# A two-layer diffusion trunk step: the end of the expert routing and the first expert, reordered

## The chip, the cores and the metric

The kernel runs on one core of one Trainium2 chip. The metric is the device time of one execution in microseconds (us); less is better. The core has a matrix engine (TensorE, PE in the rows, with its weight loads shown apart as PEld), a vector engine (VectorE, DVE), an activation engine (ScalarE, ACT), a general engine (GpSimd, POOL) and a queue engine (SyncE, SP). Each engine runs its own list of instructions in order; semaphores order them against each other. SP and POOL also start DMA transfers between the chip's memory (DRAM) and the on-chip memories.

## The reference

Two layers; each has a mixer (attention, in layer 0 beside a recurrent branch) and then an expert-choice mixture of experts with 16 experts. The change touches the mixture in both layers. 1024 latent tokens and 128 context tokens pass through the same experts in separate calls: an expert takes its 128 best latent tokens and its 16 best context tokens.

```python
def ec_moe(h, p):
    B, L, D = h.shape
    n = B * L
    cap = EC_FACTOR * n // N_EXPERTS
    xt = h.reshape(n, D)
    aff = jax.nn.softmax(jnp.matmul(xt, p['router'], preferred_element_type=jnp.float32), axis=-1)
    gate, idx = lax.top_k(aff.T, cap)
    xe = jnp.take(xt, idx, axis=0)
    hid = jax.nn.silu(jnp.einsum('ecd,edf->ecf', xe, p['w_gate'])) * jnp.einsum('ecd,edf->ecf', xe, p['w_up'])
    ye = jnp.einsum('ecf,efd->ecd', hid, p['w_down']) * gate[..., None].astype(h.dtype)
    out = jnp.zeros_like(xt).at[idx.reshape(-1)].add(ye.reshape(-1, D))
    return out.reshape(B, L, D)

def trunk_layer(x, cond, p, mixer, ctx, rope):
    sh1, sc1, g1, sh2, sc2, g2 = adaln(cond, p['ada_w'], p['ada_b'])
    mix, state = mixer(modulate(rms_norm(x, p['norm1']), sh1, sc1), p, ctx, rope)
    x = x + g1 * mix
    x = x + g2 * ec_moe(modulate(rms_norm(x, p['norm2']), sh2, sc2), p)
    return x, state
```

## The kernel before

The kernel is a row of stages. A stage is one block with a hand-written instruction list for each engine; it ends when all five engines have ended their lists. Per layer the last three stages are `mixer_out`, `routing` and `experts`.

**routing.** VectorE finds the top lists: first the context tokens' (semaphore `topped` 1), then the latent ones' in 16 rounds (`topped` 2). TensorE turns the two lists (L2164, L2165); VectorE writes them to `idx` and `gate`, and POOL gathers expert 0's 128 token rows from DRAM into `x_next` (L2022). Beside that, TensorE forms part of layer 1's modulation in `block_sums` (`ada.partial`, L260, and `ada.turn`, L248) from `ada` weights that SP loads; with `l == 0` there are ten such blocks, and the weights lie where expert weights will lie (slots 4 to 11 of `raw`). TensorE also builds the context tokens' inputs (L2153, `x_ctx`), spreads the gate vector g2 over all rows (`spread_g2`, L2131, 32 products with the identity, in the accumulator's banks 0 to 3), which ScalarE copies out (L2199), and starts expert 0's context products (`first_ctx_gu`).

**experts.** An expert's gate and up weights come in eight row blocks k of 1 MiB (`load_gu`, slots 0 to 7 of `raw`, each as two transfers of 512 KB), its down weights in four of 1 MiB (`load_dn`, slots 8 to 11). A slot is split into a high part (ScalarE, `copy_high`, L2060) and a low part (VectorE, `subtract_high`, L2063, which overwrites `raw`); TensorE then does 12 products per slot: a unit, `lat_gu` (L2449) or `lat_dn` (L2464), counted by `lat_done`. When unit k is done, SP loads the next expert's block into the slot. The context tokens use the unsplit weights: `ctx_gu` (L2051) does 32 products on four blocks of `raw`, so an expert has two halves; `ctx_dn` (L2431) does 64 on the down weights. These steps count `ctx_done`, and `low` on VectorE waits for it before it overwrites `raw`. Between them lie `turn_ctx` (L2411, transposes of the context products), `silu_ctx` on ScalarE and `hid_ctx` on VectorE. `turn_x` (L2392) transposes gathered rows, `turn_hid` (L2402) an expert's hidden rows. The loop `body(b)` runs expert b's down products and expert b+1's gate and up products.

The order in TensorE's list for expert 0, before the first `body`:

```python
            turn_x(0)
            for k in range(KB):
                lat_gu(0, k, k)
                if k == 1:
                    turn_x(1)
                    if l == 0:
                        ctx_gu(0, 1)
                if k == 5:
                    ctx_gu(1, 0)
            body(0)
```

In `body`, after the unit with k == 1, come `turn_hid(b)`, `turn_ctx(b)`, `ctx_gu(b + 1, 1)` and `ctx_dn(b)`. POOL splits expert 1's rows (`split_x`, L2342 and L2344), gathers expert 2's and then lays out expert 1's context inputs (`place_ctx`, L2044) with `l == 0`; with `l == 1` it lays them out before the split.

Of the kernel before, what the change touches and what calls it, by code (L numbers as in the profile page):

```python
# [1986 lines left out]
def moe_memory(m, a, sem, l, x_lat, h_at, hi_at, y_ctx_dram):  # L1987
# [79 lines left out]
    mm.n_low = (1, 2)[l]  # L2067
# [3 lines left out]
def routing(nc, m, a, sem, l, mm, dram, ada):  # L2071
# [16 lines left out]
    with nc.Block() as block:  # L2088
        @block.sync
        def _(sp):  # L2090
            ada.ahead(sp, (7, 3)[l])
            ada.loads(sp, (14, 0)[l])
            for k in range(4 if l == 0 else KB):
                mm.load_gu(sp, k, 0)
            if l == 1:
                for i in range(4):
                    if i < 1:
                        ada.wait_free(sp, 3 + i)
                    mm.load_dn(sp, i, 0)
# [21 lines left out]
        @block.tensor  # L2121
        def _(pe):
            def first_ctx_gu():
                pe.wait_ge(mm.s["padded"], 1)
                pe.wait_ge(mm.s["xc_ready"], 1)
                mm.ctx_gu(pe, 0, 0)

            def spread_g2():
                for c in range(2):
                    for k in range(KB):  # L2130
                        last = pe.matmul(m.psum[:, 2 * c * BANK + k * P:2 * c * BANK + (k + 1) * P],  # L2131
                                         m.mod[l][:, 5 * KB + k, c:c + 1].broadcast_to([P, P]), m.ident[:, :],
                                         start=True, stop=True)
                    last.then_inc(s["g2_spread"], 1)

            def block_sums(i):
                if i >= done:
                    ada.partial(pe, i)
                if i >= 1:
                    ada.turn(pe, i - 1)  # L2140
                if i == ada.count - 1:
                    ada.turn(pe, i)

            for i in range(early):
                block_sums(i)
            pe.wait_ge(s["sel_ready"], 1)
            for i in range(2):
                last = pe.transpose(m.psum[:, 4 * BANK + 2 * P + i * P:4 * BANK + 2 * P + (i + 1) * P], sel01[:, i, :], m.ident[:, :])
            last.then_inc(s["sel_turned"], 1)
            pe.wait_ge(s["sel_copied"], 1)  # L2150
            for k in range(KB):

                last = pe.matmul(m.psum[:, k * 2 * P:(k + 1) * 2 * P], mm.h_ctx[:, k * P:(k + 1) * P], sel_t[:, :],  # L2153
                                 start=True, stop=True)
            last.then_inc(s["ctx_done"], 1)
            for i in range(early, ada.count):
                block_sums(i)
            pe.wait_ge(s["ctx_read"], 1)
            if l == 1:
                pe.wait_ge(s["mod_ready"], 1)  # L2160
                spread_g2()
                first_ctx_gu()
            pe.wait_ge(s["topped"], 2)
            pe.transpose(m.psum[:, 4 * BANK:4 * BANK + EXP], topf[0:EXP, 0:CAP_L], m.ident[0:EXP, 0:EXP])  # L2164
            pe.transpose(m.psum[:, 4 * BANK + EXP:4 * BANK + 2 * EXP], top[0:EXP, 0:CAP_L], m.ident[0:EXP, 0:EXP]  # L2165
                         ).then_inc(s["top_turned"], 1)
            if l == 1:
                mm.ctx_gu(pe, 0, 1)
            else:
                first_ctx_gu()  # L2170
                spread_g2()

        @block.scalar
        def _(act):
            for i in range(early):
                ada.copy(act, i)
            if l == 1:
                for k in range(2):
                    act.wait_ge(mm.loaded[k], 32)
                    mm.copy_high(act, k)  # L2180
# [16 lines left out]
            for c in range(2):  # L2197
                act.wait_ge(s["g2_spread"], c + 1)
                act.copy(mm.g2[:, c, :], m.psum[:, 2 * c * BANK:(2 * c + 2) * BANK]).then_inc(s["g2_read"], 1)  # L2199
            if l == 1:  # L2200
                act.wait_ge(mm.s["ctx_done"], 2)
                mm.copy_gu_c(act)
# [64 lines left out]
def experts(nc, m, a, sem, l, mm, dram, x_ctx_from, x_ctx_to, tail_loads):  # L2267
# [20 lines left out]
    with nc.Block() as block:  # L2288
        @block.sync
        def _(sp):  # L2290
# [19 lines left out]
            if l == 0:  # L2310
                for k in range(4, KB):
                    mm.load_gu(sp, k, 0)
# [25 lines left out]
        def _(pool):  # L2338
# [17 lines left out]
            def body(b, first=False, more=2):  # L2356
                if not first:
                    scatter(b - 1)
                if more >= 1:
                    wait_value(m, pool, s["ctx_done"], b * 3 + 4)  # L2360
# [6 lines left out]
            if l == 1:  # L2367
                mm.place_ctx(pool, 1)
# [15 lines left out]
        def _(pe):  # L2384
# [83 lines left out]
            def body(b, last=False):  # L2468
                for k in range(KB):
                    lat_gu(b + 1, b * UNITS + (8 + k), k)  # L2470
                    if k == 1:
                        turn_hid(b)
                        turn_ctx(b)
                        ctx_gu(b + 1, 1)
                        ctx_dn(b)
# [12 lines left out]
            turn_x(0)  # L2488
            for k in range(KB):
                lat_gu(0, k, k)  # L2490
                if k == 1:
                    turn_x(1)
                    if l == 0:
                        ctx_gu(0, 1)
                if k == 5:
                    ctx_gu(1, 0)
            body(0)
# [14 lines left out]
        def _(act):  # L2512
# [29 lines left out]
            def read_gu_c(e):  # L2542
                act.wait_ge(s["ctx_done"], e * 3 + 1 if not (isinstance(e, int) and e == 0) else 2)
# [12 lines left out]
            def body(b, last=False):  # L2556
# [14 lines left out]
                silu_ctx(b)  # L2571
# [30 lines left out]
            if l == 0:  # L2602
                read_gu_c(0)
            for k in (6, 7):
                high(k, 32, k - 3)
            for k in (0, 1, 2):
# [3 lines left out]
            body(0)  # L2610
# [7 lines left out]
        def _(dve):  # L2618
# [38 lines left out]
            def body(b, first=False, more=True, last=False):  # L2657
# [5 lines left out]
                hid_ctx(b)  # L2663
                hid_low(b)
                for n in (4, 5, 6, 7):
                    low(unit(n), n, b * 3 + 4)
# [29 lines left out]
            for k in range(4, 8):  # L2696
                low(k, k, 2)
                if k == 5:
                    next_rows(2)
            for k in range(2):  # L2700
# [133 lines left out]
```

## Time and profile before

| what | us |
|---|---|
| median of 3 runs | 3346.57 |
| lowest and highest run | 3341.72 and 3347.82 |
| the profiled execution | 3345.91 |
| its span, first to last instruction | 3344.1 |
| TensorE busy in the span | 3125.9 (93%) |
| VectorE, ScalarE, GpSimd busy | 2259.8, 1887.1, 629.0 |

All times in the rows are from the span's start. Layer 0's routing stage runs from 748.4 to 802, its experts from 802.8; layer 1's routing from 2537.7 to 2585, its experts from 2586. A row of the timeline gives start, duration, engine, line, operation, output and inputs, the number of instructions merged into it, and in brackets the idle time of the engine just before it with what ended that. A merged row runs from the first start to the last end; matmuls overlap, so the time that a step takes is read from its start to the next row's start.

### The profile page before, as it was taken

The page shows a single profiled execution, that of the slowest core. Times are in us where ns is not written, and L with a number is a line of the kernel's source. Part 1 is how long each engine was busy: PE and PEld are TensorE (multiplying, and loading weights), DVE is VectorE, ACT ScalarE, POOL GpSimd, SP SyncE. Part 2 cuts the span into 40 slices and gives each one's busy share as a digit, 9 for nine tenths or more (in the row PEclk, how much of TensorE's full clock was granted, in tenths as well). Part 3 has the DMA queues.
Part 4 walks back from the last instruction along what each step waited for, and adds up shares of the span by engine and source line. Part 5 has one row for each costly group of instructions (what it writes and reads, how often), then busy time and mean ns, then how long its engine had stood idle before and what let it go on. Part 6 is the DMA issues. An engine that isn't in the chain of part 4 may idle for free. (4 is left out here: it accounts for less than half of the span.)

```text
span 3344.1 us, 55681 instructions
## 1 busy us (share of the span) xinstructions
PE 3125.9 (93%) x20174; PEld 2419.7 (72%) x20174; DVE 2259.8 (68%) x2853; ACT 1887.1 (56%) x2677; POOL 629.0 (19%) x484
## 2 busy tenths in 40 slices
PE   6988989988999999997999999999996999999999
PEld 4757878864677776775787888888884667677676
DVE  4667777547566666665687786867757666666666
ACT  3545848434466656664366483855733565566654
POOL 1111010001222233221211111021100222322221
PEclk9989999998999999998999999999997999999999
DMA  6230000349788888886010100100145788888885
GB/s 230 87 129 21 2 22 1 135 168 355 261 308 288 305 285 287 309 288 203 7 42 8 42 5 4 42 7 23 46 164 201 264 302 289 285 306 291 302 287 160
DMA packets 214171, 565.37 MB, mean 169 GB/s; under 512 B 33699, under 2 KB 71272, under 8 KB 213736
## 3 DMA queue, kind: packets, MB, share of 16 engines
q1 hardware_dynamic: 203614, 529.21, 43.8%
q0 software_dynamic: 9472, 33.57, 4.2%
q8 instruction: 110, 1.80, 0.2%
q14 instruction: 69, 0.57, 0.0%
q10 hardware_dynamic: 906, 0.23, 0.0%
HBM read 524.00 MB, written 38.94 MB: 168 GB/s over the span
## 5 line engine op out<-in xcount | busy, mean ns | idle before, releaser
L2063 DVE TENSOR_TENSOR moe_lo<-moe_raw,moeg_hi 128x2048 fp32r<-128x2048 f32 x384 | 883.5, 2328 | 308.3 <-ACT moeg_hi L2060 164.2
L2060 ACT CAST moeg_hi<-moe_raw 128x2048 fp32r<-128x2048 f32 x384 | 729.2, 1911 | 460.0 <-PE psum L2449 338.7
L1090 PE MATMUL psum<-attn_w_hi,attn_hs 128*128 128x256 f32 (+2 forms) x1440 | 375.0, 344 | 30.5 <-PEq L2726 14.6
L1575 DVE TENSOR_REDUCE attn_neg_max<-psum 128x1 f32<-128x1280 f32 (+1 forms) x216 | 292.5, 1354 | 86.5 <-PE psum L1196 85.4
L1196 PE MATMUL psum<-attn_ks,attn_qst 128*128 128x512 f32 (+2 forms) x1200 | 313.1, 377 | 21.8 <-ACT attn_e L1356 12.4
L1356 ACT ACTIVATE attn_e<-psum,attn_neg_max 128x1280 f32<-128x1280 f32 (+1 forms) x216 | 264.8, 1226 | 75.8 <-DVE attn_neg_max L1575 55.1
L1090 PEld LDWEIGHTS psum<-attn_w_hi,attn_hs 128*128 128x128 f32 x1440 | 254.8, 191 | 62.5 <-issue 21.9
L2449 PE MATMUL psum<-moeg_hi,moeh_x_hi 128*128 128x512 f32 x960 | 261.8, 394 | 4.8 <-issue 4.8
L2449 PE MATMUL psum<-moe_lo,moeh_x_hi 128*128 128x512 f32 x960 | 263.5, 396 | 0.0
L2449 PE MATMUL psum<-moeg_hi,moeh_x_lo 128*128 128x512 f32 x960 | 262.0, 394 | 0.0
L1090 PE MATMUL psum<-attn_w_lo,attn_hs 128*128 128x512 f32 (+2 forms) x720 | 244.6, 340 | 0.0
L2051 PE MATMUL psum<-moe_raw,moeh_xc 128*32 128x512 f32 x2048 | 236.8, 602 | 7.0 <-DMA moe_raw<-in_l_w_up 5.9
L1196 PEld LDWEIGHTS psum<-attn_ks,attn_qst 128*128 128x128 f32 x1200 | 200.4, 190 | 52.7 <-ACT attn_e L1356 20.6
L2449 PEld LDWEIGHTS psum<-moeg_hi,moeh_x_hi 128*128 128x128 f32 x960 | 178.0, 188 | 55.4 <-issue 18.0
L1290 ACT COPY attn_pt<-psum 128x512 f32<-128x512 f32 (+2 forms) x400 | 191.7, 506 | 37.8 <-PE psum L1209 29.6
L2449 PEld LDWEIGHTS psum<-moeg_hi,moeh_x_lo 128*128 128x128 f32 x960 | 181.3, 189 | 42.7
L2449 PEld LDWEIGHTS psum<-moe_lo,moeh_x_hi 128*128 128x128 f32 x960 | 181.3, 189 | 41.4
L1209 PE MATMUL psum<-ident,attn_e 128*128 128x128 f32 x1296 | 198.1, 279 | 11.5 <-ACT attn_pt L1290 5.7
L1209 PEld LDWEIGHTS psum<-ident,attn_e 128*128 128x128 f32 x1296 | 145.5, 141 | 44.6 <-issue 25.1
L1072 POOL TENSOR_TENSOR rstd<-ssq,neg_half 128x8 f32<-128x8 f32 (+1 forms) x54 | 80.1, 1483 | 498.5 <-DVE ssq L1481 498.5
L2044 POOL COPY moeh_xc<-moe_x_ctx 128x64 f32 (+1 forms) x64 | 125.6, 1994 | 227.0 <-PE psum L2051 201.4
L1238 PE MATMUL psum<-attn_v,attn_pt 128*128 128x128 f32 x1296 | 158.1, 276 | 5.7 <-ACT attn_pt L1290 4.3
(350 smaller groups left out, 5398.8 us busy)
## 6 DMA issues: line engine op xcount, KB each, us to landing
moe_raw<-in_l_w_gate SPq DMA_DIRECT2D x256, 512.0 KB, 4.1
moe_raw<-in_l_w_up SPq DMA_DIRECT2D x256, 512.0 KB, 5.1
moe_raw<-in_l_w_down SPq DMA_DIRECT2D x128, 1024.0 KB, 6.1
ada_w<-in_l_ada_w SPq DMA_DIRECT2D x23, 1024.0 KB, 14.2
ada1h_w<-in_l_ada_w SPq DMA_DIRECT2D x9, 1024.0 KB, 10.6
lru_ada<-in_l_ada_w SPq DMA_DIRECT2D x8, 1024.0 KB, 6.3
lru_late<-in_l_ada_w SPq DMA_DIRECT2D x8, 1024.0 KB, 11.4
out_w<-in_l_w_out SPq DMA_DIRECT2D x16, 512.0 KB, 5.4
```

What stands on the lines that cost most here:

```text
L1090: last = pe.matmul(out, hs[t % 2][:, part, k, :], right, start=(i == 0 and n == 0), stop=(i == KB - 1 and n == 2))
L1196: last = pe.matmul(m.psum[:, into:into + step], qst[(u // per_tile) % 2][:, qm, v, :], ks[:, km, col:col + step], start=(v == 0), stop=(v ...
L1209: last = pe.transpose(m.psum[:, at + (i - b) * P:at + (i - b + 1) * P], src[:, i * P:(i + 1) * P], m.ident[:, :])
L1238: last = pe.matmul(m.psum[:, at:at + dv], pt[u % 2][:, i * P:(i + 1) * P], vt[:, kt, col:col + dv], start=(i == 0), stop=(i == len(tiles) ...
L1290: act.copy(out, src).then_inc(s["turn_read"], 1)
L1356: act.activation(out[:, 0:hi - lo], m.psum[:, score_at(n):score_at(n) + hi - lo], ACT.Exp, bias=neg_max[:, n:n + 1], accum_out=sums[:, n:n ...
L1575: dve.tensor_reduce(neg_max[:, n:n + 1], m.psum[:, score_at(n):score_at(n) + hi - lo], AX.X, ALU.max, negate=True).then_inc(s["maxed"], 1)
L2044: last = pool.tensor_copy(dst[:, :, j, :], mm.x_ctx[:, :, ds(e * 8 + j * P, 8)])
L2051: last = pe.matmul(m.psum[32 * g:32 * g + 32, 6 * BANK:7 * BANK], mm.xc[:, k, :], mm.raw[k][:, g // 2, (g % 2) * BANK:(g % 2 + 1) * BANK], ...
L2060: act.copy(mm.hi[slot % 4][:, :, :], mm.raw[slot][:, :, :]).then_inc(mm.s["hi_ready"], 1)
L2063: dve.tensor_tensor(mm.lo[slot][:, :, :], mm.raw[slot][:, :, :], mm.hi[slot % 4][:, :, :].bitcast(F32), ALU.subtract).then_inc(mm.s["lo_re ...
L2449: last = pe.matmul(m.psum[:, at:at + BANK], x[:, k, :], w[:, j, half * BANK:(half + 1) * BANK], start=(k == 0 and i == 0), stop=(k == KB - ...
```

## The change

In `routing` with `l == 0`: SP issues the loads of blocks 4 to 7 of expert 0 here (after the `ada` weights in those slots have been used) instead of at the start of `experts`; `spread_g2` and its copies run after the third `block_sums` instead of at the end; the lists are turned after the last `ada.partial` and ahead of the last two `ada.turn`; the first half of expert 0's context products and the first low part move to `experts`. With `l == 1`: the second half of expert 0's context products, with its copy, and the second low part move to `experts`. In `experts`: these context products run right after `turn_x(0)`; `turn_ctx(0)` runs after unit 4, and `ctx_dn(0)` between expert 0's last gate and up unit and `body(0)`, whose first pass leaves both out; the waits on `ctx_done` follow the new order.

```diff
@@ moe_memory
-    mm.n_low = (1, 2)[l]
+    mm.n_low = (0, 1)[l]
@@ routing, block.sync
-            for k in range(4 if l == 0 else KB):
+            for k in range(KB):
+                if l == 0 and k >= 4:
+                    ada.wait_free(sp, k - 1)
                 mm.load_gu(sp, k, 0)
@@ routing, block.tensor
             def block_sums(i):
                 if i >= done:
                     ada.partial(pe, i)
+                if i == ada.count - 1 and l == 0:
+                    turn_lists()
                 if i >= 1:
                     ada.turn(pe, i - 1)
                 if i == ada.count - 1:
                     ada.turn(pe, i)
+            def turn_lists():
+                pe.wait_ge(s["topped"], 2)
+                pe.transpose(m.psum[:, 4 * BANK:4 * BANK + EXP], topf[0:EXP, 0:CAP_L], m.ident[0:EXP, 0:EXP])
+                pe.transpose(m.psum[:, 4 * BANK + EXP:4 * BANK + 2 * EXP], top[0:EXP, 0:CAP_L], m.ident[0:EXP, 0:EXP]
+                             ).then_inc(s["top_turned"], 1)
             for i in range(early):
                 block_sums(i)
+                if i == 2 and l == 0:
+                    spread_g2()
...
             pe.wait_ge(s["sel_copied"], 1)
+            if l == 0:
+                pe.wait_ge(s["g2_read"], 2)
...
             for i in range(early, ada.count):
                 block_sums(i)
-            pe.wait_ge(s["ctx_read"], 1)
             if l == 1:
+                pe.wait_ge(s["ctx_read"], 1)
                 pe.wait_ge(s["mod_ready"], 1)
                 spread_g2()
                 first_ctx_gu()
-            pe.wait_ge(s["topped"], 2)
-            pe.transpose(m.psum[:, 4 * BANK:4 * BANK + EXP], topf[0:EXP, 0:CAP_L], m.ident[0:EXP, 0:EXP])
-            pe.transpose(m.psum[:, 4 * BANK + EXP:4 * BANK + 2 * EXP], top[0:EXP, 0:CAP_L], m.ident[0:EXP, 0:EXP]
-                         ).then_inc(s["top_turned"], 1)
-            if l == 1:
-                mm.ctx_gu(pe, 0, 1)
-            else:
-                first_ctx_gu()
-                spread_g2()
+                turn_lists()
@@ routing, block.scalar
+            def read_g2():
+                for c in range(2):
+                    act.wait_ge(s["g2_spread"], c + 1)
+                    act.copy(mm.g2[:, c, :], m.psum[:, 2 * c * BANK:(2 * c + 2) * BANK]).then_inc(s["g2_read"], 1)
             for i in range(early):
                 ada.copy(act, i)
+                if i == 2 and l == 0:
+                    read_g2()
...
-            for c in range(2):
-                act.wait_ge(s["g2_spread"], c + 1)
-                act.copy(mm.g2[:, c, :], m.psum[:, 2 * c * BANK:(2 * c + 2) * BANK]).then_inc(s["g2_read"], 1)
             if l == 1:
-                act.wait_ge(mm.s["ctx_done"], 2)
-                mm.copy_gu_c(act)
+                read_g2()
@@ experts, block.sync
             if l == 0:
-                for k in range(4, KB):
-                    mm.load_gu(sp, k, 0)
                 for i in range(4):
                     mm.load_dn(sp, i, 0)
@@ experts, block.gpsimd
-                    wait_value(m, pool, s["ctx_done"], b * 3 + 4)
+                    wait_value(m, pool, s["ctx_done"], 5 if first else b * 3 + 4)
...
             if l == 1:
+                pool.wait_ge(s["ctx_done"], 2)
                 mm.place_ctx(pool, 1)
@@ experts, block.tensor
-            def body(b, last=False):
+            def body(b, first=False, last=False):
                 for k in range(KB):
                     lat_gu(b + 1, b * UNITS + (8 + k), k)
                     if k == 1:
                         turn_hid(b)
-                        turn_ctx(b)
+                        if not first:
+                            turn_ctx(b)
                         ctx_gu(b + 1, 1)
-                        ctx_dn(b)
+                        if not first:
+                            ctx_dn(b)
...
             turn_x(0)
+            pe.wait_ge(s["padded"], 1)
+            ctx_gu(0, l)
             for k in range(KB):
                 lat_gu(0, k, k)
                 if k == 1:
                     turn_x(1)
                     if l == 0:
                         ctx_gu(0, 1)
+                if k == 4:
+                    turn_ctx(0)
                 if k == 5:
                     ctx_gu(1, 0)
-            body(0)
+            ctx_dn(0)
+            body(0, first=True)
@@ experts, block.scalar
-                act.wait_ge(s["ctx_done"], e * 3 + 1 if not (isinstance(e, int) and e == 0) else 2)
+                act.wait_ge(s["ctx_done"], e * 3 + 1 if not (isinstance(e, int) and e <= 1) else 3 * e + 2)
...
             read_x(1)
-            if l == 0:
-                read_gu_c(0)
+            read_gu_c(0)
             for k in (6, 7):
                 high(k, 32, k - 3)
+            silu_ctx(0)
@@ experts, block.vector
-                hid_ctx(b)
+                if not first:
+                    hid_ctx(b)
                 hid_low(b)
                 for n in (4, 5, 6, 7):
-                    low(unit(n), n, b * 3 + 4)
+                    low(unit(n), n, 5 if first else b * 3 + 4)
...
+            hid_ctx(0)
             for k in range(2):
                 low(KB + k, k, 3)
```

## Rows read from the trace of the kernel before

**Rows 1.** Windows: length, busy (instructions) of PE, PEld, DVE, ACT, POOL, PEclk, DMA, GB/s.
```profile
797.00:803.00 6.00, 4.13 (x38) 3.87 (x35) 2.29 (x1) 2.03 (x2) 0.00 (x0) 1.00 0.01 1
...
820.00:832.00 12.00, 10.98 (x48) 8.57 (x46) 11.77 (x5) 5.46 (x5) 11.41 (x5) 1.00 1.02 408
...
862.00:910.00 48.00, 48.00 (x312) 33.51 (x308) 32.62 (x20) 28.65 (x26) 13.72 (x6) 1.00 0.74 272
```

**Rows 2.** Timeline, layer 0, end of routing: start, duration, engine, line, operation, [idle before].
```profile
789.89 1.95 PE L248 MATMUL psum<-fold,ada1s_row 128*128 128x2 f32 x16
...
791.76 0.23 PE L2164 MATMUL psum<-ident,route_topf 16*128 16x16 f32 x1
...
792.54 1.05 POOL L2022 DMA_INDIRECT moe_x_next<-h_rows,moe_idx_now  x1 [5.84 <-DVE moe_idx_now L2255]
...
797.10 3.84 PE L2131 MATMUL psum<-ident,mod 128*128 128x128 f32 x32
...
800.97 1.01 ACT L2199 COPY moe_g<-psum 128x1024 f32<-128x1024 f32 x1 [0.77 <-PE psum L2131]
802.76 0.33 SPq L2013 DMA_DIRECT2D moe_raw<-in_l_w_gate  x1
```

**Rows 3.** Timeline, layer 0, first expert, up to its sixth unit and the block behind it.
```profile
807.50 2.08 PE L2449 MATMUL psum<-moeg_hi,moeh_hid_hi 128*128 128x512 f32 x4 [3.63 <-DVE moeh_hid_lo L2692]
...
815.07 1.03 PE L2392 MATMUL psum<-ident,moe_x_next 128*128 128x128 f32 x8
...
816.03 3.64 PE L2051 MATMUL psum<-moe_raw,moeh_xc 128*32 128x512 f32 x32
...
830.42 1.63 POOL L2044 COPY moeh_xc<-moe_x_ctx 128x64 f32<-128x64 f32 x2
...
839.84 1.93 PE L2051 MATMUL psum<-moe_raw,moeh_xc 128*32 128x512 f32 x8 [1.50 <-DMA moe_raw<-in_l_w_up]
```

**Rows 4.** Timeline, layer 0, from the second expert's first unit to its third.
```profile
851.82 1.35 PE L2449 MATMUL psum<-moeg_hi,moeh_x_hi 128*128 128x512 f32 x4 [2.42 <-issue]
...
856.23 1.09 PE L2449 MATMUL psum<-moeg_hi,moeh_x_hi 128*128 128x512 f32 x4
...
859.00 1.04 PE L2402 MATMUL psum<-ident,moeh_hid_rows 128*128 128x128 f32 x8
...
863.86 3.64 PE L2431 MATMUL psum<-moe_raw,moeh_hid_c 128*32 128x256 f32 x64
...
867.43 1.19 PE L2449 MATMUL psum<-moeg_hi,moeh_x_hi 128*128 128x512 f32 x4
```

**Rows 5.** Windows, TensorE at its lower clock before the second expert.
```profile
852.70:856.00 3.30, 3.30 (x10) 2.53 (x9) 3.30 (x2) 1.35 (x1) 0.00 (x0) 0.50 0.69 273
```

**Rows 6.** Timeline, layer 1, end of routing and first expert.
```profile
2578.84 5.77 PE L2051 MATMUL psum<-moe_raw,moeh_xc 128*32 128x512 f32 x32
...
2580.57 4.50 DVE L2063 TENSOR_TENSOR moe_lo<-moe_raw,moeg_hi 128x2048 fp32r<-128x2048 f32 x2 [1.30 <-POOL route_pair L2119]
...
2586.10 1.06 PE L2392 MATMUL psum<-ident,moe_x_next 128*128 128x128 f32 x8 [1.48 <-PEq L2726]
...
2590.84 2.07 PE L2449 MATMUL psum<-moeg_hi,moeh_hid_hi 128*128 128x512 f32 x4 [3.68 <-DVE moeh_hid_lo L2692]
...
2638.69 1.19 PE L2449 MATMUL psum<-moeg_hi,moeh_x_hi 128*128 128x512 f32 x4
```

**Rows 7.** Timeline, layer 0, a wait for ada weights in the middle of routing.
```profile
761.27 1.93 PE L260 MATMUL psum<-ada_w,cond 128*32 128x512 f32 x8 [5.17 <-DMA ada_w<-in_l_ada_w]
```

**Rows 8.** DMA issues, us to landing: gathers of 792.54, 804.85, 2579.40; weights of 825.91.
```profile
moe_x_next<-h_rows,moe_idx_now POOLq DMA_INDIRECT x1, 5.7
...
moe_x_next<-h_rows,moe_idx_now POOLq DMA_INDIRECT x1, 8.7
...
moe_x_next<-h_rows,moe_idx_now POOLq DMA_INDIRECT x1, 4.4
...
moe_raw<-in_l_w_up SPq DMA_DIRECT2D x1, 512.0 KB, 13.9
```

More of the change, by code:

```diff
@@ L2554, in silu, with body @@
                 act.activation(mm.act[:, :], m.psum[:, 0:2 * BANK], ACT.Silu).then_inc(s["silu_done"], 1)
-            def body(b, last=False):
+            def body(b, first=False, last=False):
                 def step(n):
@@ L2570, in body @@
                     step(n)
-                silu_ctx(b)
+                if not first:
+                    silu_ctx(b)
                 hid_high(b)
@@ L2609, in _ @@
                 high(k, 64, KB + k - 3)
-            body(0)
+            body(0, first=True)
             with act.Fori(1, LAST - 1) as b:
@@ L2662, in body @@
                     low(unit(n), n, b * 3 + 3)
-                hid_ctx(b)
+                if not first:
+                    hid_ctx(b)
                 hid_low(b)
                 for n in (4, 5, 6, 7):
-                    low(unit(n), n, b * 3 + 4)
+                    low(unit(n), n, 5 if first else b * 3 + 4)
                 for n in (8, 9):
```

## Prediction

> **What bounds the kernel now.** I read the windows view by stage first. From 862 on, in the loop over experts, TensorE is busy 48.00 of 48.00 us while DMA moves 272 GB/s; where DMA is the limit it moves 408 [rows 1]. So the loop is TensorE's, and a shift of its start is a shift of everything behind it. The change touches only what lies ahead of that loop, once per layer, so I looked there for idle time. The windows show the first hole: from 797 to 803, DMA moves 1 GB/s [rows 1]. All that SyncE had issued in routing has landed, and the next load waits for the stage to end. The timeline of that end shows why it ends late: expert 0's context products, then the gate spread of 3.84 us, then two copies, the last from 800.97 to 801.98; 0.78 later the next stage begins at 802.76 [rows 2]. The timeline of the first expert shows who pays: TensorE waits in the context block of expert 1 for weights that land only at 839.84; that block ends at 841.77 [rows 3]. Then it waits 2.42 us for SiLU and product, and the next unit takes 4.41 us (851.82 to 856.23) in place of 2.77 (856.23 to 859.00) [rows 4], because the granted clock had fallen to 0.50, the 1.2 GHz level, behind that wait [rows 5]. I measure by one mark: the start of expert 1's third gate-and-up unit, 867.43 in layer 0 [rows 4] and 2638.69 in layer 1 [rows 6]. Behind it nothing idles.
>
> **Layer 0, end of routing.** Moved away: the spread, its copies, the first context half, the first low part. The lists now follow the last ada products, at 789.89 and not at 791.76, so 1.87 earlier [rows 2]. The two folds behind them still take 1.95, so TensorE ends at about 792.3; VectorE's modulation sums follow (some 0.7) and end the stage at about 793.0; with the 0.78 the next begins at **793.8**, 9.0 earlier. SyncE's four more loads wait for ada slots; the last of these is used when the last block but one is done, about 787, so SyncE does not end the stage. Queued behind that wait on SyncE is nothing but the down loads of the next stage.
>
> The spread goes to the third block. Its cover is the wait for ada weights there, 5.17 us [rows 7], against 3.84 warm and 3.84 x 5.77/3.64 = 6.1 at the lower clock [rows 2, 3, 6]: cost 0 to 0.9, and that rest meets further waits for the same loads. I take 0; without the cover it would be 3.84 to 6.1. ScalarE's copies sit behind the spread while nothing else is due there.
>
> **Layer 0, the gather.** It starts 0.78 after the lists [rows 2]: at 790.7. It took 5.7 us when the weight queue ran dry behind it, 8.7 beside a full one and 4.4 with an empty one [rows 8]. Now the queue stays full, so I take 9 (8.7 and a margin): landed at **799.7**. The first transposes wait for it, so of the 9.0 us only 802.8 - 799.7 = 3.1 is left; the context block is queued behind them on TensorE and cannot fill the wait.
>
> **Layer 0, up to the mark.** Transposes 1.06 [rows 6]; context half, 3.64 warm [rows 3], 5.77 after an idle stretch [rows 6], taken as 5.3, since TensorE idles some 7 us before: 806.1. The low part of block 0 waits for it (`ctx_done`), 2.25 each [rows 6] and 0.25 for the hand-over: the first unit at **808.6**, 1.1 later than the 807.50 of before [rows 3]. Two units: 7.57 before (807.50 to 815.07 [rows 3]), 5.54 warm; I take 7.2: 815.8. Then turn_x 0.96 and context half 3.57 (815.07, 816.03 [rows 3], and its length as the 3.57 from 863.86 to 867.43 [rows 4] of the same work), four units 11.08, turn_ctx 0.5 (four transposes, of which eight take 1.03 [rows 3]): 831.9. The next block waits for POOL: its layout ended 832.05 - 815.07 = 17.0 after this point before [rows 3], so 832.8. Then 3.57, two units 5.54, `ctx_dn` 3.57, two units 5.54, turn_hid and a context half 4.86 - 0.5 = 4.4 (859.00 to 863.86 without turn_ctx [rows 4]): the mark at 855.4. **Layer 0: -12.0.** `ctx_dn` is not less work; it stands in the 2.42 us hole, and since TensorE then does not idle, the 4.41 us unit becomes 2.77.
>
> Does DMA keep up? At 408 GB/s [rows 1] 1 MiB takes 2.57. From 797: blocks 4 to 7, 10.3; two gathers of 512 KB, 2.6; down weights 10.3: 820.2. Expert 1's blocks 0 and 1 are issued before that, blocks 2 and 3 as units end, at about 823 and 826; four blocks land by about 831, ahead of 832.8. So DMA has some 2 us in hand, and no earlier start in layer 0 can give much over 3 us more. That SyncE issues blocks 4 to 7 in routing is worth little by itself: at 793.8 the queue would still hold 3 us of work.
>
> **Layer 1.** Routing's end loses the context half and the second low part: VectorE ends at 2580.57 + 2.25 = 2582.8; the next stage begins at 2583.6. The gather landed at 2583.8 [rows 8, 6]. So the transposes start at 2583.8, 2.3 earlier than 2586.10 [rows 6]. The context half then runs in the time in which ScalarE and VectorE prepare the rows, 2590.84 - 2586.10 = 4.74 with the transposes [rows 6]; transposes and block are 1.06 + 5.3, so the first unit starts at 2590.2, 0.6 earlier. But TensorE has worked without a break and is warm: two units 5.6. With turn_x 0.8, 11.08, 0.5, 3.57, 5.54, 3.57, 5.54 and 4.4 the mark is at 2630.8. **Layer 1: -7.9.** The added wait of POOL (`ctx_done` 2) holds back the layout and the split of expert 1's rows, and behind them the next gather; the split's user comes some 30 us later, cost 0.
>
> **The sum.** 12.0 + 7.9 = 19.9 off the profiled execution's 3345.9 (its span 3344.1; the rest lies outside and is not touched; the median of the runs is 0.7 above it): **3326.0**.
>
> **Bounds.** No row shows the clock that the moved blocks will get. Warm from the start, context half 3.64 and units 2.77: 3.3 more off in layer 0 (no more, as DMA binds), 1.7 in layer 1. At the lower clock throughout: 32 products take 6.8 (1.93 for 8 less their overlap, 1.7 each [rows 3]), units at 4.41 [rows 4]: 3.1 less in layer 0, 3.8 in layer 1. Together 3321 to 3333.
>
> **The rivals.** *The loads keep their age.* Expert 1's weights took 13.9 us from issue to landing [rows 8] as they stood behind 8 MiB. If they still do, though issued at 823 and 826, the last lands at 840 and the block ends at 842, as before: layer 0 keeps only the hole and the two slow stretches, 6, and layer 1 its 7.9: 3332. Against it: the queue has only the down weights ahead by then, and DMA was idle 6 us that it now uses [rows 1].
>
> *The gather lands sooner*, after 5.7 as in the row of before [rows 8]: 3.3 earlier, all of it usable: 3322.7. Against it are the 8.7 beside a full queue. The Trainium skill (DMA: Bandwidth & Descriptors, section Queues, rings and completion order) speaks for it: each DMA engine takes turns between the queues packet by packet, so a gather would wait for no backlog. With the fixed 2.0 us of that page's section on the anatomy of a DMA and twice 1.3 for the halved rate that is an estimate of 4.6, so by the page the sum would be about 3322; the measured 8.7 is well above it, and I go by that.
>
> *Slower: the lower clock holds.* The change puts TensorE's first work behind a wait of 7 us in layer 0 and 5 in layer 1. If the clock then stays at 1.2 GHz through both first experts, each unit costs 4.41 - 2.77 = 1.64 more [rows 4]; there are 20 gate-and-up units up to the marks, 33 us, against 19.9 gained: 3359. It breaks even at 12 such units and is slower by 0.2% from 16. Against it: before, TensorE was back at the full clock within one or two units of steady work each time [rows 4, 5].
>
> *Given back.* The loop takes the earlier start and loses it to another engine: within 0.2%, 3345. Against it: in the loop VectorE is busy 33, ScalarE 29 and POOL 14 of 48 us [rows 1].
>
> **How the numbers follow.** Forecast 0.70, 3326 with its bounds. Loads keep their age 0.13. Gather sooner 0.08. Given back 0.06. Slower 0.03. About 0.2%, 6.7 us, is what a measurement of this kernel can tell from no change. Faster is the first three, 0.91; same 0.06; slower 0.03. The range takes in the bounds, the first two rivals and the spread of the runs, some 3 us each way: 3319 to 3337.
>
> **What would show it.** In the changed profile: the DMA hole of 797 to 803 is gone; layer 0's experts stage begins near 794 with TensorE idle until 799 to 800; the first unit is not earlier than before in layer 0; no wait for weights at expert 1's block; no 2.42 us hole before the second expert's first unit, and that unit at 2.8 us; the marks some 12 and 8 us earlier. Wrong would be: a wait on DMA in that block, a first unit after 812, or a loop with idle TensorE.

## The result, and the profile after

| | before | after |
|---|---|---|
| median, us (lowest to highest of 5 runs each) | 3347.09 (3341.72 to 3351.68) | 3328.44 (3328.07 to 3333.97) |
| ratio, 95% interval | | 0.9947 (0.9937 to 0.9957) |
| span of the profiled execution | 3344.1 | 3326.6 |
| layer 0: start of routing to the mark | 867.43 - 748.40 = 119.03 | 856.21 - 750.48 = 105.73 |
| mark to the start of layer 1's routing | 1670.26 | 1669.80 |
| layer 1: start of routing to the mark | 2638.69 - 2537.69 = 101.00 | 2620.97 - 2526.01 = 94.96 |
| mark to the end | 705.4 | 705.6 |

The forecast was 3326.0, from 3319 to 3337: it holds, and the kernel is faster. The mark is the start of the second expert's (expert 1's) third gate-and-up unit; the start of routing is the start of its first GpSimd instruction. What lies ahead of layer 0's routing was not touched, and varies from trace to trace (it ended between 746.5 and 753.8 in all traces of this study), so I compare stretches, not times of day. They give -13.3 and -6.0 where I said -12.0 and -7.9. The span fell by 17.5, and not by 19.3, mostly because routing started 2.1 later in this trace. What lies between layer 0's mark and layer 1's routing was not touched either; it takes 1666.9 to 1670.9 in all traces, so its -0.46 here says nothing.

The windows of the changed kernel (length, busy time and instructions of PE, PEld, DVE, ACT, POOL, granted clock, DMA share, GB/s):

```profile
797.00:803.00 6.00, 2.38 (x12) 1.77 (x16) 0.41 (x3) 0.41 (x2) 0.00 (x0) 0.50 1.03 410
820.00:832.00 12.00, 12.00 (x59) 9.32 (x52) 11.14 (x5) 8.72 (x10) 10.37 (x4) 1.00 0.94 348
...
852.00:900.00 48.00, 48.00 (x284) 33.05 (x286) 33.23 (x21) 31.75 (x28) 13.74 (x7) 1.00 0.83 299
```

The hole in DMA of [rows 1] is gone (410 GB/s for 1), and the loop still has TensorE busy 48.00 of 48.00. The timeline of the changed kernel at layer 0's end of routing (start, duration, engine, line, operation, idle before):

```profile
791.51 0.23 PE L2150 MATMUL psum<-ident,route_topf 16*128 16x16 f32 x1
...
792.25 1.09 SPq L2013 DMA_DIRECT2D moe_raw<-in_l_w_up  x1
792.28 1.05 POOL L2022 DMA_INDIRECT moe_x_next<-h_rows,moe_idx_now  x1 [3.96 <-DVE moe_idx_now L2264]
...
794.03 0.26 DVE L291 SCALAR_TENSOR_TENSOR norm_scale<-mod,vec_a 128x16 f32<-128x16 f32 x2
800.57 3.16 SPq L2018 DMA_DIRECT2D moe_raw<-in_l_w_down  x4
800.62 1.94 PE L2400 MATMUL psum<-ident,moe_x_next 128*128 128x128 f32 x8 [6.94 <-PEq L2744]
802.49 5.43 PE L2051 MATMUL psum<-moe_raw,moeh_xc 128*32 128x512 f32 x32
```

Every list has ended by 794.3, yet the next stage (SP's down loads) begins at 800.57, not near 794. The DMA issues say what came 0.84 before it: the gather of 792.28 took 7.4, so it landed at 799.7.

```profile
moe_x_next<-h_rows,moe_idx_now POOLq DMA_INDIRECT x1, 7.4
```

Then the first expert:

```profile
810.51 1.15 PE L2457 MATMUL psum<-moeg_hi,moeh_hid_hi 128*128 128x512 f32 x4 [2.59 <-DVE moe_lo L2063]
...
816.12 1.03 PE L2400 MATMUL psum<-ident,moe_x_next 128*128 128x128 f32 x8
...
833.15 3.64 PE L2051 MATMUL psum<-moe_raw,moeh_xc 128*32 128x512 f32 x32 [0.71 <-POOL moeh_xc L2044]
836.72 1.19 PE L2457 MATMUL psum<-moeg_hi,moeh_hid_hi 128*128 128x512 f32 x4
...
842.45 3.66 PE L2439 MATMUL psum<-moe_raw,moeh_hid_c 128*32 128x256 f32 x64
...
846.04 1.20 PE L2457 MATMUL psum<-moeg_hi,moeh_x_hi 128*128 128x512 f32 x4
...
856.21 1.19 PE L2457 MATMUL psum<-moeg_hi,moeh_x_hi 128*128 128x512 f32 x4
```

Against [rows 3, 4]: the context block of expert 1 waits 0.71 for GpSimd and not for DMA, and neither the 2.42 us wait nor the unit of 4.41 us is there. Layer 1, against [rows 6]:

```profile
2572.89 1.94 PE L2400 MATMUL psum<-ident,moe_x_next 128*128 128x128 f32 x8 [5.78 <-PEq L2744]
2574.76 5.05 PE L2051 MATMUL psum<-moe_raw,moeh_xc 128*32 128x512 f32 x32
...
2579.74 1.20 PE L2457 MATMUL psum<-moeg_hi,moeh_hid_hi 128*128 128x512 f32 x4
...
2585.39 1.03 PE L2400 MATMUL psum<-ident,moe_x_next 128*128 128x128 f32 x8
...
2620.97 1.19 PE L2457 MATMUL psum<-moeg_hi,moeh_x_hi 128*128 128x512 f32 x4
```

### The profile page after: what moved, and what is told of

The parts are those of the page before. It is cut to its first block and busy times, and to the rows that moved or that the text cites. A ratio compares the mean times of both kernels' runs of the same rounds, so it can differ in the third digit from the quotient of the medians.

```text
span 3326.6 us, 55683 instructions
## 1 busy us (share of the span) xinstructions
PE 3119.5 (94%) x20174; PEld 2419.2 (73%) x20174; DVE 2258.6 (68%) x2853; ACT 1886.3 (57%) x2677; POOL 630.9 (19%) x484
## 5 line engine op out<-in xcount | busy, mean ns | idle before, releaser
L1356 ACT ACTIVATE attn_e<-psum,attn_neg_max 128x1280 f32<-128x1280 f32 (+1 forms) x216 | 264.7, 1226 | 75.7 <-DVE attn_neg_max L1575 54.9
```

Source lines behind the costliest of these rows:

```text
L1356: act.activation(out[:, 0:hi - lo], m.psum[:, score_at(n):score_at(n) + hi - lo], ACT.Exp, bias=neg_max[:, n:n + 1], accum_out=sums[:, n:n ...
```

## The experiments

The table gives the stretches from the start of routing to the mark, from one trace per kernel, and the ratio to the kernel before from runs on the same chip. Three traces leave the changed layer 0 as it is (after, e6, e10: 105.73 to 106.59) and six the changed layer 1 (94.80 to 95.42), so a difference under 0.9 us in layer 0, or under 0.7 in layer 1, tells nothing. Most of that spread lies ahead of the experts stage: from the first transposes to the mark, layer 0 takes 55.60, 55.66 and 55.73 in after, e10 and e6.

| kernel | layer 0 | layer 1 | ratio (95%) |
|---|---|---|---|
| before | 119.03 | 101.00 | 1 |
| after | 105.73 | 94.96 | 0.9947 (0.9937 to 0.9957) |
| e10, after once more | 106.59 | 95.42 | 0.9943 (0.9929 to 0.9956) |
| e1, after, blocks 4 to 7 late | 107.58 | 95.30 | 0.9948 (0.9930 to 0.9967) |
| e2, after, down products back | 108.52 | 97.71 | 0.9958 (0.9946 to 0.9971) |
| e4, after, gather in experts | 108.88 | 94.80 | one run, 3332.41 us |
| e5, after, context half in the wait | 105.01 | 95.18 | 0.9941 (0.9927 to 0.9954) |
| e6, after, layer 1's start back | 106.43 | 96.97 | 0.9948 (0.9933 to 0.9964) |
| e9, e5 and the next wait filled | 102.12 | 95.15 | 0.9936 (0.9922 to 0.9949) |
| e3, before, loads alone | 114.49 | 100.57 | 0.9974 (0.9964 to 0.9983) |
| e11, e3 once more | 109.69 | 100.92 | 0.9968 (0.9953 to 0.9982) |
| e7, before, down products alone | 115.55 | 97.15 | 0.9978 (0.9968 to 0.9987) |
| e8, before, spread alone | 116.13 | 101.08 | 0.9994 (0.9985 to 1.0004) |

**What ends the stage (e4).**

```diff
-            pool.wait_ge(s["idx_ready"], 1)
-            mm.gather(pool, dram)
+            if l == 1:
+                ...
...
@@ experts, block.gpsimd
+            if l == 0:
+                mm.gather(pool, dram)
             gather(1)
```

> The changed kernel, but in layer 0 GpSimd starts the gather of expert 0's rows at the start of the experts stage and not in routing. In the changed kernel the experts stage begins at 800.6, 50.1 us behind the start of routing, though TensorE, VectorE and SyncE have ended their lists by 793.3 to 794.6; the gather lands at 799.7. My theory (a stage does not end before the gather that it started has landed): the stage now begins within 1 us of the last list's end, at about 44 to 45 us behind the start of routing; the gather then lands some 8 us later, TensorE starts the transposes 52 to 54 behind, and the mark comes 2 to 4 us later than in the changed kernel. Rival (the stage's end waits for something else, a load or an engine that the trace does not show): the stage still begins about 50 us behind, and the mark comes some 8 us later.

The semaphore that GpSimd raises behind the gather, and VectorE's wait for it, go with the gather in layer 0; in after that wait was over by 793.5. The timeline of e4 at the same place:

```profile
795.64 8.70 SPq L2018 DMA_DIRECT2D moe_raw<-in_l_w_down  x4
796.37 1.05 POOL L2022 DMA_INDIRECT moe_x_next<-h_rows,moe_idx_now  x1 [7.46 <-POOLq L2748]
804.07 1.97 PE L2404 MATMUL psum<-ident,moe_x_next 128*128 128x128 f32 x8 [9.80 <-DMA moe_x_next<-h_rows,moe_idx_now]
```

The stage begins 795.64 - 751.14 = 44.5 behind the start of routing, for 50.1 with the gather in routing. The theory holds: this stage does not end before its gather has landed. In all seven traces with the changed layer 0 and the gather in routing, the next stage begins 0.84 to 0.97 behind the landing. Which instruction at the end of the stage waits for it is not shown. The mark comes 2.3 to 3.2 later, since the gather starts later.

**The early loads (e1; e3 and e11 alone).** In e1:

```diff
-            for k in range(KB):
-                if l == 0 and k >= 4:
-                    ada.wait_free(sp, k - 1)
+            for k in range(4 if l == 0 else KB):
                 mm.load_gu(sp, k, 0)
@@ experts, block.sync
             if l == 0:
+                for k in range(4, KB):
+                    mm.load_gu(sp, k, 0)
```

> The changed kernel, but SyncE issues expert 0's blocks 4 to 7 in layer 0 at the start of the experts stage again, as before the change. My theory (the early issue is worth little by itself, 0 to 1 us): the gather no longer stands beside a full weight queue, lands in about 5.7 us and not 7.4, so the stage begins some 1.7 us sooner; a stretch of about 4 us in which DMA moves nothing comes back ahead of it; from the start of layer 0's routing to the second expert's third gate-and-up unit 105.7 us, -1.7 to +1.0, and no wait of TensorE for weights at expert 1's context block. Rival (the early issue is what removed the wait for weights): the missing 4 MiB push expert 1's weights late again, that block waits 1.5 us or more for DMA, and the stretch is 4 to 8 us longer, 110 to 114.

Its window before the stage, and its block of expert 1:

```profile
800.00:804.00 4.00, 0.15 (x1) 0.18 (x2) 0.00 (x0) 0.00 (x0) 0.00 (x0) 0.50 0.21 82
```

```profile
840.85 1.07 PE L2051 MATMUL psum<-moe_raw,moeh_xc 128*32 128x512 f32 x8 [1.45 <-DMA moe_raw<-in_l_w_up]
```

DMA runs nearly dry from 800 to 804, and the wait for weights comes back at 1.45: my expectation (no wait) failed, and the rival's mechanism is there at less than half of its lowest price, 4. The gather landed no sooner (49.2 behind the start of routing in both). The stretch is 1.0 to 1.9 longer; from the first transposes to the mark it is 57.53, 1.8 to 1.9 longer than in after, e10 and e6. The ratios can't show so little.

e3 is the same edit the other way round, on the kernel before:

> The kernel before with one part of the change alone: in layer 0's routing SyncE issues blocks 4 to 7 of expert 0 as soon as their slots are free. The experts stage begins where it did, 54.4 us behind the start of routing, since TensorE and ScalarE still end it. My theory (with the stage late, the loads are what the first expert lacks): 4 MiB land while DMA moved nothing before, expert 1's weights land some 6 us earlier, its context block no longer waits for DMA and ends about 6 us earlier, and what stood behind it keeps its hole of 2.4 us: layer 0's stretch 119.0 - 6 to 8 = 111 to 113, layer 1 unchanged at 101.0, in all about 3339. Rival (the loads are hidden anyway, as my sum said for the changed kernel): 119.0 within 1, 3346.

> The kernel before with the early loads alone, unaltered, for a second trace. Its first trace shows 4.5 us less in layer 0's stretch and 0.4 in layer 1's, its median 8.7 less. If the trace is typical: 114.5 and 100.6 again, the stage 58.7 behind the start of routing. If the context products wait less for their weights in other executions: the stage at 54 to 56 and the mark at 110 to 112.

The two traces differ at the end of routing. First e3, then e11:

```profile
801.32 1.93 PE L2051 MATMUL psum<-moe_raw,moeh_xc 128*32 128x512 f32 x8 [2.47 <-DMA moe_raw<-in_l_w_up]
803.18 5.92 PE L2133 MATMUL psum<-ident,mod 128*128 128x128 f32 x32
```

```profile
795.76 1.07 PE L2051 MATMUL psum<-moe_raw,moeh_xc 128*32 128x512 f32 x8 [1.44 <-DMA moe_raw<-in_l_w_up]
796.76 3.84 PE L2133 MATMUL psum<-ident,mod 128*128 128x128 f32 x32
```

In e3 the context half waits longer for its weights, and the spread behind it takes 5.92 for 3.84, at a granted clock of 0.50 up to 806; so the stage begins 4.3 later than before, in e11 only 0.4 later. Behind the start of the stage both gain: 55.8 and 54.9 to the mark, for 119.03 - 54.41 = 64.6 before. So the loads alone are worth some 9 in the first expert, and can lose half of it in routing as long as the context half and the spread stand behind them there. The change takes both away. Why the blocks landed later in the first trace is not shown. The first trace is not typical: its run took 3345.56, and the median of e3's ten is 3338.93; over all of them e3 is 0.26% or 8.7 us faster than the kernel before, near the 9.3 of e11's stretch.

**The down products (e2 back, e7 alone).** e2:

```diff
@@ body, k == 1
                         ctx_gu(b + 1, 1)
-                        if not first:
-                            ctx_dn(b)
+                        ctx_dn(b)
@@
-            ctx_dn(0)
             body(0, first=True)
```

> The changed kernel, but expert 0's context down products stand in the first pass of the loop again, behind the context block of expert 1's second half, in both layers; its transposes and everything else stay where the change put them. My theory (the products fill a hole and keep the clock up): TensorE waits some 2.4 us for SiLU and product ahead of expert 1's... second expert's first unit, and the unit behind the wait takes 4.41 and not 2.77, since the granted clock falls to 0.50: about 4 us more per layer, the layer 0 stretch from routing to the mark 105.7 + 4 = 109.7, layer 1 95.0 + 4 = 99, in all 3336.5. Rival (the hole is closed anyway, since the earlier loads let SiLU and product end sooner): no wait, clock at 1.00, both stretches the same within 0.7 us.

e7 is the kernel before with `turn_ctx(0)` behind unit 4 and `ctx_dn(0)` ahead of `body`:

> The kernel before with one part of the change alone, in both layers: expert 0's context down products stand between its last gate-and-up unit and the loop, their transposes behind unit 4. Theory of the prediction (the 2.42 us wait lowers the clock, so closing it makes the unit of 4.41 us one of 2.77): 4.05 less in each layer, the marks at 115.0 and 97.0 in place of 119.0 and 101.0. Rival, from the run that put the products back and found the wait without a lower clock behind it: the wait alone, 2.8 in each layer, with a slow unit still there: 116.2 and 98.2.

e2's first unit of the second expert, with the window over this unit:

```profile
845.03 1.17 PE L2457 MATMUL psum<-moeg_hi,moeh_x_hi 128*128 128x512 f32 x4 [2.41 <-issue]
```

```profile
845.03:847.80 2.77, 2.77 (x12) 2.29 (x13) 2.30 (x2) 2.24 (x2) 0.00 (x0) 1.00 0.99 386
```

The wait is there, 2.41, and the clock stays at 1.00 behind it: putting the products back costs 1.9 to 2.8 in layer 0 and 2.3 to 2.9 in layer 1, not 4. From the first transposes of layer 0 it costs 2.3 to 2.4, the wait alone. On the kernel before, moving the products alone gives 3.5 and 3.85, near the 4.05 expected: in the kernel before the slow unit did go with the wait (in e7 it takes 851.88 to 854.77, 2.89). So the wait costs 2.4 for sure, and the 1.6 of the slow unit only where the clock falls behind it. It fell in the kernel before and in e8 (both layers), and in layer 1 of e3 and e11; it did not in e2 (both layers) or in layer 0 of e3 and e11, behind the same 2.41 or 2.42. In layer 0 it thus fell only in the traces in which expert 1's context block had waited for weights shortly before (before, e8). No such wait sets the traces of layer 1 apart, so what decides it stays open.

**The spread (e8).**

```diff
             for i in range(early):
                 block_sums(i)
+                if i == 2 and l == 0:
+                    spread_g2()
...
                 first_ctx_gu()
-                spread_g2()
...
```

> The kernel before with one part of the change alone: in layer 0 the gate spread and its two copies stand behind the third block of modulation products. Theory (a wait for weights covers the spread there): the lists are turned no later than 43.4 us behind the start of routing; the stage ends with the low part of block 0, the next begins at 51.5 to 52 in place of 54.4; the loads that it issues come that much sooner, so the wait for them at expert 1's block shrinks by as much, and the mark comes 2.5 earlier, at 116.5. Rival (the cover is not there): up to 6 us more ahead of the lists, and the mark at 119 to 122.

```profile
756.09 3.82 PE L2131 MATMUL psum<-ident,mod 128*128 128x128 f32 x32
759.84 1.07 PE L260 MATMUL psum<-ada_w,cond 128*32 128x512 f32 x8
762.48 1.07 PE L260 MATMUL psum<-ada_w,cond 128*32 128x512 f32 x8 [1.57 <-DMA ada_w<-in_l_ada_w]
```

The wait for modulation weights that covered 5.17 [rows 7] is 1.57 behind the spread, and the stretch is 2.9 shorter, as expected. The timing (0.9985 to 1.0004) neither confirms nor denies so little.

**Layer 1's start (e6).**

```diff
+    mm.n_low = (0, 2)[l]
@@ routing, layer 1, at the end of TensorE's and ScalarE's lists
+                mm.ctx_gu(pe, 0, 1)
+                act.wait_ge(mm.s["ctx_done"], 2)
+                mm.copy_gu_c(act)
...
```

> The changed kernel, but in layer 1 the second half of expert 0's context products, its copy and the second low part stand at the end of routing again, as before. Theory (working without a break behind the transposes keeps TensorE's clock up, and that is the gain of this part): the transposes start some 1.2 to 2.3 us later and the first unit at 53.2 us behind the start of routing in place of 53.7; TensorE waits 3.7 between; the first two units take 8.4 and not 5.65; layer 1's mark at 97.0 to 97.5 in place of 95.0; in all +2.2. Rival (the clock comes up anyway): two units at 5.6 and the mark 0.5 earlier than in the changed kernel.

```profile
2578.05 2.08 PE L2460 MATMUL psum<-moeg_hi,moeh_hid_hi 128*128 128x512 f32 x4 [3.68 <-DVE moeh_hid_lo L2714]
...
2586.41 1.03 PE L2403 MATMUL psum<-ident,moe_x_next 128*128 128x128 f32 x8
```

As the theory said: the first unit comes 0.7 earlier (53.04 for 53.73), the two units take 8.36 for 5.65, and the mark comes 1.6 to 2.2 later. From 2578.05 to 2583.30 the granted clock is 0.50, the 1.2 GHz level. This part of the change gives no earlier start; it gives the clock.

**Clock or DMA in layer 0 (e5, e9, e10).** e5 moves the first context half back into routing, and so into TensorE's wait for the gather; e9 adds filler work:

```diff
@@ e5: routing, layer 0, behind the last block_sums
+                first_ctx_gu()
@@ e5: experts, block.vector, l == 0, first thing
+                low(0, 0, 1)
@@ e9: experts, block.tensor, l == 0, behind turn_x(0)
+                for k in range(32):
+                    pe.transpose(m.psum[:, 7 * BANK + (k % 4) * P:7 * BANK + (k % 4 + 1) * P], m.ident[:, :], m.ident[:, :])
...
```

> The changed kernel, but in layer 0 the first half of expert 0's context products stands in routing again, behind the last products of the modulation, where TensorE waits 6.9 us for the gather; VectorE does the low part of block 0 first thing in the experts stage. Theory of the prediction (DMA binds, so no earlier start gives much over 3 us): first gate-and-up unit at 56.2 us behind the start of routing in place of 60.0; two units at the lower clock, 7 to 8.4 and not 5.6, take half of it back; expert 1's context block waits up to 1.5 for weights; the mark at 102.5 to 105.2 in place of 105.7. Rival (the start of the first unit sets the mark): all 3.8 come through, 102 or less, and no wait on DMA. Third case (the products in routing wait for blocks 0 to 3 and end the stage late): stage later than 50.1 and the mark at 106 or more.

> The kernel with the context products in TensorE's wait, and 32 transposes of the identity matrix into an accumulator bank that nothing reads at that time, in the 4.79 us in which TensorE there waits ahead of its first unit in layer 0. Two theories are told apart. First, that the wait is what lowers the clock: the two first units take 5.6 and not 8.5. Second, on the 2.9 us that this frees: my prediction said that DMA binds (no earlier start gives much over 3 us); then expert 1's context block, which now waits 0.70 for GpSimd with its last weights landed 81.2 us behind the start of routing, waits for DMA instead and the mark comes at 104.2 to 104.8 in place of 105.0. Rival (DMA has room): all 2.9 come through, the mark at 102.1. If the clock stays low in spite of the transposes: mark 105 to 106.

> The changed kernel once more, unaltered, beside the others on one chip: its stretches as before, 105.7 and 95.0 within 0.7, its time 0.52% to 0.54% under the kernel before; against it the version with the context products in the wait should be 0.7 us shorter by its trace, which is under what timing can tell.

e5, then e9, from the first unit to the second turn of rows, each with a window over these units (the granted clock is the third number from the end), and e9's block of expert 1:

```profile
805.25 2.08 PE L2459 MATMUL psum<-moeg_hi,moeh_hid_hi 128*128 128x512 f32 x4 [4.79 <-DVE moeh_hid_lo L2714]
...
813.77 1.04 PE L2402 MATMUL psum<-ident,moe_x_next 128*128 128x128 f32 x8
```

```profile
805.00:811.00 6.00, 5.75 (x14) 4.50 (x15) 6.00 (x4) 3.26 (x3) 0.00 (x0) 0.50 1.03 412
```

```profile
801.66 3.66 PE L2506 MATMUL psum<-ident 128*128 128x128 f32 x32
806.62 1.20 PE L2459 MATMUL psum<-moeg_hi,moeh_hid_hi 128*128 128x512 f32 x4 [1.30 <-DVE moeh_hid_lo L2717]
...
812.28 1.04 PE L2402 MATMUL psum<-ident,moe_x_next 128*128 128x128 f32 x8
...
829.32 3.64 PE L2051 MATMUL psum<-moe_raw,moeh_xc 128*32 128x512 f32 x32 [0.69 <-POOL moeh_xc L2044]
```

```profile
801.00:812.00 11.00, 9.70 (x63) 8.50 (x62) 10.85 (x12) 9.45 (x9) 0.97 (x1) 1.00 1.03 410
```

In e5 the first unit is 3.7 earlier and 2.9 of it goes to the clock: two units take 8.52 for 5.61. In e9, with transposes that compute nothing, they take 5.66, and all of it comes through: 102.12, 3.6 to 4.5 under the changed kernel. Expert 1's block still waits for GpSimd, not for DMA. Both questions are answered: the wait lowers the clock here, and DMA does not bind yet. In e9 the last weights of that block land at 830.43, 1.1 behind its start; but only its last quarter uses them ([rows 3] show that quarter as the one that waits), some 2.7 behind the start, so about 1.6 us of room are left. The other traces agree about the first question: over both layers of all 13, TensorE waits 3.62 to 4.79 right ahead of expert 0's first unit in 12 cases, and the two units then take 7.34 to 8.52; in the other 14 cases work stands there, at most 2.60 of the wait is left, and they take 5.61 to 5.68. e9 beats the kernel before (0.9936); against the changed kernel beside it (0.9943) the intervals overlap, so its gain over that kernel rests on the trace.

## Why the prediction was right, point by point

By steps, in us (the rows of before that [rows 3, 4, 6] lack stand below the table):

| step | before | forecast | after |
|---|---|---|---|
| layer 0: start of routing to the first unit | 59.10 | 60.2 | 60.03 |
| two units | 7.57 | 7.2 | 5.61 |
| to the end of expert 1's context block | 26.64 | 20.6 | 20.60 |
| to the mark | 25.72 | 19.0 | 19.49 |
| layer 1: start of routing to the first unit | 53.15 | 52.5 | 53.73 |
| two units | 8.39 | 5.6 | 5.65 |
| to the mark | 39.46 | 35.0 | 35.58 |

```profile
841.71 2.08 PE L2449 MATMUL psum<-moeg_hi,moeh_hid_hi 128*128 128x512 f32 x4
...
2599.23 1.03 PE L2392 MATMUL psum<-ident,moe_x_next 128*128 128x128 f32 x8
```

In the points, times of after are set back by 2.08 in layer 0 and put forward by 11.68 in layer 1, so that routing starts where it did before.

- **Bound and mark: right.** Between and behind the marks the time changed by -0.46 and +0.2; nothing was given back.
- **Lists turned 1.87 earlier: right** (789.43 for 789.89 said), and the spread's cover held (e8).
- **Next stage at 793.8: wrong**, 798.49. I let the slowest list and 0.78 end the stage, as if a stage ended with its five lists, and left out that the gather must have landed (e4). It cost the sum nothing, since the transposes wait for the same gather: said 799.7, measured 798.5, as the gather took 7.4 for 9 and the stage's start took 0.9 of that back.
- **First unit in layer 0 at 808.6: right by luck**, 808.43, with errors that cancel: the transposes began 1.2 sooner, took 1.87 for 1.06, as the granted clock was 0.50 (window 797 to 803), and from the context half to the first unit it took 8.02 for 7.8.
- **Two units at 7.2: wrong, and the source of layer 0's surplus** (1.6 of it; 0.3 was lost elsewhere). They took 5.61: the granted clock was back at 1.00 from 806, while the context block ahead of them ran.
- **Context block of expert 1 waits for GpSimd, not DMA: right**, at 831.07 for 832.8. Its last weights landed 1.25 ahead of its start (831.90 and 833.15 in the trace), for 1.8 said. The two blocks issued at 823.79 or later took 4 to 5 us, so they were not old: the first rival is out.
- **The early issue is "worth little by itself" (0 to 1 in e1's expectation): too low**, and by the wrong stage start: at 793.8 the queue would have held work; at 800.6 it has run dry when the loads are late (e1: 82 GB/s, then a wait of 1.45). The early issue is worth 1.0 to 1.9 here, and alone some 9 in the first expert (e11).
- **No more than 3 us beyond this, as DMA binds: the size near, the reason wrong.** e9 gave 3.6 to 4.5 with DMA still not last; I had counted the last weights as needed at the block's start, and its last quarter uses them.
- **The down products: right in sum, split wrongly.** The wait and the slow unit make 4.05 on the kernel before (e7: 3.5 and 3.85), but only the 2.4 of the wait is sure (e2).
- **Layer 1, -7.9: too much**, -6.0. The first unit came at 2591.42 for 2590.2: the stage again began behind the landed gather (+0.8), and the transposes took 1.87 for 1.06. Two units 5.65 for 5.6: right, and e6 shows that they are the gain. Behind them it took 35.58 for 35.0: the steps are slightly longer than the shortest rows that I took for them.
- **Bounds.** One was summed wrongly: at the lower clock throughout, layer 1's own terms give (6.8 - 5.3) + (8.82 - 5.6) = 4.7 more and not 3.8, so the bounds end at 3334; nothing else rests on it.
- **The lower clock: it did not hold**, and came back at 806.
- **The sooner gather: it did not come.** It took 7.4 to 9.0 in traces with a full weight queue, and 4.1 to 5.1 with an empty one.

The trace of after shows where the gather's time goes. None of its packets moves before 796.5, 4.3 behind the issue; with an empty queue the first moves 1.8 behind it. From 796.5 to 799.3 all 144 move, beside 0.62 MB of weights (q1 is SyncE's queue, q0 the gather's; packets, MB, share of the DMA engines):

```profile
q1 hardware_dynamic: 171, 0.62, 55.8%
q0 software_dynamic: 144, 0.52, 46.9%
```

The Trainium skill (DMA: Bandwidth & Descriptors, section Queues, rings and completion order) has each engine take turns between queues. These rows agree with that for the time in which the packets move. The estimate of 4.6 added the fixed 2.0 us of that page's section on the anatomy of a DMA; beside a full weight queue the late start of the first packet makes that part too small. Why it starts late is not shown.

In all the gain was 1.3 larger in layer 0 and 1.9 smaller in layer 1, so the stretches miss the sum by 0.6 only because two errors nearly cancel. With the 2.1 by which routing started later in the profiled run, less 0.3 elsewhere, that is the 2.4 between 3326.0 and 3328.4.

## What to carry to other kernels

Where TensorE must wait ahead of dense matmuls, try independent matmuls in the wait that stands last before them: here that took 2.7 to 2.9 us off the next two units, and in layer 1 it was worth more than a start that came 0.7 sooner (e6). The stages here that had started a gather ended only after it had landed, so count the landing among the lists that end such a stage. Price a moved load with the stage times that the change really gives: the same four loads were worth some 9 us, or 1 to 2, depending on what else the change had already moved.

## What the runs showed of the hardware

- Behind a stage that had started a gather on GpSimd, the next stage began 0.84 to 0.97 after the landing (seven traces of layer 0), in after with every list done 6.3 us earlier; without the gather it began 5.6 earlier (e4).
- 32 transposes of the identity, whose results nothing reads, kept the granted clock at 1.00, the 2.4 GHz level, through the first two units: 5.66 for 8.52.
- The same wait of 2.41 us was followed by the 1.2 GHz level in six stretches (before and e8 in both layers, e3 and e11 in layer 1) and not in four (e2 in both layers, e3 and e11 in layer 0).
- A gather of 512 KB from 128 rows took 4.1 to 5.1 with the weight queue empty, 4.8 to 6.9 as it ran dry, 7.4 to 9.0 beside a full one. Beside a full queue its first packet moved 4.1 to 4.7 behind the issue, for 1.7 to 1.8 with an empty one.
